# Both K ranges of the ups as seven products in a two-layer decoder trunk

## Chip, cores, metric

One core of one Trainium2 chip runs the whole program. The metric is the device time of one execution in microseconds. Engines: TensorE (PE) multiplies and writes PSUM, ScalarE (ACT), VectorE (DVE) and GpSimd (POOL) compute, SyncE (SP) issues most of the transfers. All arrays in memory are float32.

## What is computed

Two layers over 256 tokens of width 2048: a mixer and a SwiGLU feed-forward part with a residual each. The mixers aren't touched. The feed-forward part of each layer is

```
FFN_HIDDEN = 5632
def swiglu(h, w_gate, w_up, w_down):
    return (jax.nn.silu(h @ w_gate) * (h @ w_up)) @ w_down
h = rms_norm(x, ffn_norm[layer])
x = x + swiglu(h, w_gate[layer], w_up[layer], w_down[layer])
```

## The kernel before

**Numbers.** Every float32 operand is split in two halves that the fast matmul format holds: hi is the operand rounded, lo is the operand minus hi. A product of two operands is hi*hi + hi_w*lo_a + lo_w*hi_a, three matmuls in place of one.

**Slots.** The weights are read as blocks of 512 rows by 512 columns (1 MB), held as 128 x 2048. Each use of a block or of a sum of blocks is a *slot*. For slot t the SP queue loads the block into a place, ACT casts it to hi (`prepare`, line 807), DVE makes lo (line 1173), and PE multiplies. hi and lo have three places each, so the cast of slot t waits until PE has used slot t - 3, and on ACT and DVE `prepare(s + 3)` stands behind what belongs to step s. The blocks themselves lie in four places of `raw` and two of `work`; a load waits until the lo that frees its place is made.

**Units.** The hidden width is 11 units of 512 columns. The feed-forward part of each layer runs in five groups: FIRST (the first unit, steps g and h, and a pair of units), three times MIDDLE (a pair each), and LAST (a pair). What happens in a group is a list of steps, written out by hand at the top of the file; it sets the order on every engine. In it a0 to a5 and b0 to b5 with x0 and x1 are the gate projection of the pair, u, q and r the up projection, e, d and D the down projection (of the first unit, of the pair before, of the last pair), and T0, T1, t0, t1 are *turns*: PE transposes a finished unit, ACT rounds it to hi, DVE takes lo.

**Seven products.** For a pair of units, two halves of the tokens (128 each) and two K tiles of 512, the output is a 2 x 2 product of blocks, W11 to W22 of the weights. It is computed with seven products in place of eight: the products use W11, W22, W21 and sums of blocks, and the results are combined by small DVE operations of 128 x 512 (`gates`, `ups`) and kept in PSUM banks. The K range of 2048 is two such ranges: a is the first (K rows 0 to 1023) and b the second, x0 and x1 the seventh product of each. A product is one slot with 12 matmuls of 512 columns. A *wide* slot (g, h, e, d, D, q, r, v, w) uses one block for both token halves, with 24 matmuls.

The ups of FIRST and MIDDLE use seven products for the first K range only (u0 to u6); the second is done with four wide slots (q0, q1, r0, r1). The ups of LAST are eight wide slots (v, w).

**Sums of blocks.** DVE adds blocks in place right after the lo of slots 0, 1 and 3 of a range (line 1180). For a and b the sums with W12 are made by transfers from POOL's queue that add to the block in SBUF (`add_block`, line 759); for u W12 is loaded plainly and DVE adds it (`ADDED_BY_DMA`, `SOURCE`, `w12_loaded`). Per MIDDLE that is 33 slots, 8 sums on DVE, 25 loads from SP and 4 adding transfers from POOL.

**Waits that matter.** Small DVE operations of a group wait until PE has used their slot. T0 and T1 wait for the last of them that their unit needs. The down steps d00 and on wait until the turned unit is taken (`turn_taken`).

## Time and profile before

| | us |
|---|---|
| median of 3 runs | 1890.61 (1890.18 to 1891.11) |
| profiled execution | 1890.08 |
| its span | 1888.3 |
| PE busy | 1879.0 (100%) |
| PEld (weight loads) busy | 1583.5 (84%) |
| DVE busy | 1528.4 (81%) |
| ACT busy | 1000.2 (53%) |
| POOL busy | 80.0 (4%) |
| DMA | 414.49 MB, mean 220 GB/s |

Busy time is the time in which at least one instruction of the engine runs. A matmul's duration reaches over the start of the next one, so that the distance of two starts tells what one costs; on DVE too the next operation starts a little before the last has ended.

### The profile page before, as it was taken

The page shows a single profiled execution, that of the slowest core. Times are in us where ns is not written, and L with a number is a line of the kernel's source. Part 1 is how long each engine was busy: PE and PEld are TensorE (multiplying, and loading weights), DVE is VectorE, ACT ScalarE, POOL GpSimd, SP SyncE. Part 2 cuts the span into 40 slices and gives each one's busy share as a digit, 9 for nine tenths or more (in the row PEclk, how much of TensorE's full clock was granted, in tenths as well). Part 3 has the DMA queues.
Part 4 walks back from the last instruction along what each step waited for, and adds up shares of the span by engine and source line. Part 5 has one row for each costly group of instructions (what it writes and reads, how often), then busy time and mean ns, then how long its engine had stood idle before and what let it go on. Part 6 is the DMA issues. An engine that isn't in the chain of part 4 may idle for free.

```text
span 1888.3 us, 22147 instructions
## 1 busy us (share of the span) xinstructions
PE 1879.0 (100%) x9142; PEld 1583.5 (84%) x9142; DVE 1528.4 (81%) x1139; ACT 1000.2 (53%) x771; POOL 80.0 (4%) x125
## 2 busy tenths in 40 slices
PE   9999999999999999999999999999999999999998
PEld 8889999988888888888888888888888888888886
DVE  6656788966699899898897757889989899898855
ACT  6444344445555565555554536756565565555534
POOL 1000000000000000001000400010000000000000
PEclk9999999999999999999999999999999999999999
DMA  9555445355697868878878755497986868868762
GB/s 305 194 175 174 146 155 161 140 190 167 195 286 246 231 223 266 254 250 221 278 223 239 249 203 179 161 229 256 261 287 226 228 223 263 251 249 235 246 228 89
DMA packets 231772, 414.49 MB, mean 220 GB/s; under 512 B 6449, under 2 KB 55682, under 8 KB 231426
## 3 DMA queue, kind: packets, MB, share of 16 engines
q1 hardware_dynamic: 210336, 370.71, 56.3%
q0 software_dynamic: 21120, 41.95, 13.2%
q8 instruction: 67, 1.10, 0.2%
q10 hardware_dynamic: 226, 0.55, 0.1%
q14 instruction: 23, 0.19, 0.0%
HBM read 411.08 MB, written 2.10 MB: 219 GB/s over the span
## 4 chain that ended last, share of the span: by engine, by line
PE 97%; DVE 1%; DMA 1%; ACT 0%; issue 0%; SPq 0%; DVEq 0%; ACTq 0%
PE main L1844 28%; PE main L1850 14%; PE aux L1866 11%; PE main L1786 8%; PE main L1866 7%; PE aux L1870 6%; PE main L1788 4%; PE main L1870 3%; PE main L2083 3%; PE aux L2083 3%; PE main L2089 2%; PE aux L2089 1%; PE aux L1961 1%; PE aux L1793 1%; PE main L1894 1%; PE main L1893 1%
## 5 line engine op out<-in xcount | busy, mean ns | idle before, releaser
L807 ACT CAST hi<-raw 128x2048 fp32r<-128x2048 f32 (+1 forms) x328 | 624.5, 1907 | 503.1 <-PE main L1850 227.6
L1173 DVE TENSOR_TENSOR lo<-raw,hi 128x2048 fp32r<-128x2048 f32 x255 | 581.1, 2288 | 119.6 <-ACT hi L807 119.5
L1844 PE MATMUL main<-hi,mid 128*128 128x512 f32 x1632 | 387.8, 390 | 0.5 <-ACT hi L807 0.5
L1844 PEld LDWEIGHTS main<-hi,mid 128*128 128x128 f32 x1632 | 305.5, 188 | 63.9 <-issue 0.9
L807 ACT CAST hi<-work 128x2048 fp32r<-128x2048 f32 (+2 forms) x102 | 191.2, 1877 | 145.7 <-PE main L1850 26.6
L1173 DVE TENSOR_TENSOR lo<-work,hi 128x2048 fp32r<-128x2048 f32 x97 | 221.6, 2286 | 43.7 <-ACT hi L807 43.7
L1786 PE MATMUL main<-act,hi 128*128 128x512 f32 x640 | 226.6, 397 | 0.0
L1165 DVE TENSOR_TENSOR lo<-raw,hi 128x2048 fp32r<-128x2048 f32 x71 | 162.4, 2290 | 71.8 <-ACT hi L807 71.8
L1850 PE MATMUL main<-lo,mid 128*128 128x512 f32 x816 | 201.6, 389 | 0.0
L1850 PEld LDWEIGHTS main<-lo,mid 128*128 128x128 f32 x816 | 153.2, 188 | 31.8
L1788 PE MATMUL main<-act,lo 128*128 128x256 f32 x640 | 178.5, 279 | 0.0
L1844 PE MATMUL main<-hi,act 128*128 128x512 f32 x688 | 164.3, 391 | 0.0
L1844 PEld LDWEIGHTS main<-hi,act 128*128 128x128 f32 x688 | 128.4, 188 | 26.6 <-DVE act L1481 0.3
L1786 PEld LDWEIGHTS main<-act,hi 128*128 128x128 f32 x640 | 120.0, 188 | 26.5
L1866 PE MATMUL aux<-hi,act 128*128 128x512 f32 x544 | 136.1, 392 | 0.0
L1788 PEld LDWEIGHTS main<-act,lo 128*128 128x128 f32 x640 | 120.7, 189 | 0.3
L1866 PEld LDWEIGHTS aux<-hi,act 128*128 128x128 f32 x544 | 100.9, 188 | 20.2
L759 POOL DMA_DIRECT2D raw<-in_ffn_w_gate x31 | 40.0, 1290 | 1489.0 <-DVE lo L1173 1282.2
L1850 PE MATMUL main<-lo,act 128*128 128x512 f32 x344 | 85.0, 389 | 0.0
L1214 DVE TENSOR_TENSOR xn<-xn,main 128x1024 f32<-128x1024 f32 x55 | 66.8, 1215 | 20.6 <-PE main L1850 20.6
L1180 DVE TENSOR_TENSOR raw<-raw 128x2048 f32<-128x2048 f32 x32 | 73.0, 2285 | 6.8 <-DMA raw<-in_ffn_w_up 3.5
L1850 PEld LDWEIGHTS main<-lo,act 128*128 128x128 f32 x344 | 64.6, 188 | 13.4
(210 smaller groups left out, 2295.8 us busy)
## 6 DMA issues: line engine op xcount, KB each, us to landing
raw<-in_ffn_w_up SPq DMA_DIRECT2D x73, 1024.0 KB, 5.9
raw<-in_ffn_w_gate SPq DMA_DIRECT2D x63, 1024.0 KB, 7.0
raw<-in_ffn_w_down SPq DMA_DIRECT2D x58, 1024.0 KB, 6.6
raw<-in_ab_w_in SPq DMA_DIRECT2D x55, 1024.0 KB, 5.1
raw<-in_ffn_w_gate POOLq DMA_DIRECT2D x31, 1024.0 KB, 9.1
work<-in_ffn_w_down SPq DMA_DIRECT2D x30, 1024.0 KB, 7.5
work<-in_ffn_w_gate SPq DMA_DIRECT2D x25, 1024.0 KB, 8.0
work<-in_ffn_w_up SPq DMA_DIRECT2D x23, 1024.0 KB, 7.5
```

What stands on the lines that cost most here:

```text
L807: return nc.scalar.copy(out_, in_)
L1165: V.tensor_tensor(lo[:, s.place, :], raw[:, s.place, :], hi[:, s.place, :].bitcast(F32), ALU.subtract).then_inc(lo_ready, 1)
L1173: V.tensor_tensor(lo[:, split_at(t), :], raw_of[p.at], hi[:, split_at(t), :].bitcast(F32), ALU.subtract).then_inc(lo_ready, 1)
L1180: V.tensor_tensor(raw_of[a.at], raw_of[a.at], raw_of[b.at], ALU.add).then_inc(sum_made, 1)
L1214: V.tensor_tensor(xs, xs, bank_, ALU.add).then_inc(job_emptied, 1)
L1786: mm(bank(job)[:, c, :], hi[:, s.place, at:at + P], rhs[:, k0 + n, :, :], start=(first and n == 0), stop=False)
L1788: ins = mm(bank(job)[:, c, TOKENS:], lo[:, s.place, at:at + P], rhs[:, k0 + n, 0, :], start=False, stop=(last and n == depth - 1))
L1844: mm(o2[:, h, :], lhs[:, k0 + n, c, h * P:(h + 1) * P], w_hi, start=(first and c == 0 and n == 0), stop=False)
L1850: ins = mm(o2[:, h, :], lhs[:, k0 + n, 0, h * P:(h + 1) * P], w_lo, start=False, stop=(last and n == 3))
L1866: mm(o, a[c][:, n, :], hi[:, at, n * WIDE:(n + 1) * WIDE], start=(first and c == 0 and n == 0), stop=False)
L1870: ins = mm(o, a[0][:, n, :], lo[:, at, n * WIDE:(n + 1) * WIDE], start=False, stop=(last and n == 3))
L2083: mm(banks[:, h, :], act[:, k0 + n, c, h * P:(h + 1) * P], w_hi, start=(start[h] and c == 0 and n == 0), stop=False)
```

## The change

- The ups of all groups run as seven products over both K ranges: u0 to u5 over the first, y0 to y5 over the second, z0 and z1 the seventh products. q, r, u6, v and w are gone. Their products go to the same six banks as those of the gates, and `full_ups` combines them with 11 small operations (12 before in FIRST and MIDDLE, 4 in LAST).
- W12 of a is now loaded plainly and added by DVE (four sums on DVE); b, u and y are added by DMA (two sums on DVE each).
- W21 stays in its place unchanged: the sum for slot 5 is made in the place of W11, and x0, x1, z0 and z1 use the block that is loaded for slot 5 of the same range, without a load of their own.
- T1 (and t1) write to other banks than T0 (t0), and a3 and a4 wait for T1 to be taken, the first d waits for T0 only.
- The three lists of steps are new. Per MIDDLE there are 36 slots, 10 sums on DVE, 21 loads from SP and 6 adding transfers from POOL.

In the whole program the 512-column matmuls go from 7152 to 7008, the 128 x 2048 operations on DVE from 479 to 543, such casts on ACT from 409 to 445, and POOL's transfers from 40 to 60.

```diff
-FIRST = ("g0 g1 g2 g3 h0 h1 h2 h3 a0 T0 a2 b0 e0 a1 b2 e1 b1 a3 a4 e2 b3 a5 b5 x0 x1 b4 e3 u2 r0 u0 q0 "
-         "u1 u6 u3 q1 u4 u5 r1").split()
-MIDDLE = ("T0 a0 a2 T1 b0 b2 d00 d01 a1 x0 d10 b1 d11 a4 d20 a3 a5 x1 b3 d21 b5 b4 d30 d31 u0 u2 q0 u1 "
-          "q1 u6 u3 r0 u5 u4 r1").split()
-LAST = ("T0 a0 a2 T1 b0 b2 d00 a1 d01 a3 a5 d10 d11 b1 x0 d20 a4 d21 x1 b3 b4 b5 d30 v0 d31 v1 w0 v2 "
-        "v3 w1 t0 w2 w3 D00 t1 D10 D01 D11 D20 D21 D30 D31").split()
+FIRST = ("g0 g1 g2 g3 a0 h0 a2 a1 b0 a3 h1 a5 a4 b2 h2 b1 x0 h3 x1 T0 b3 u0 b5 b4 e0 y0 u1 z0 u2 u3 e1 "
+         "y1 u5 y2 y3 z1 u4 e2 y5 e3 y4").split()
+MIDDLE = ("a0 T0 a2 b2 d00 T1 a1 b0 a4 x0 a3 d01 a5 b1 d10 x1 b3 d11 u0 b4 b5 y0 d20 u1 u2 u3 z0 u5 d21 "
+          "y1 y2 y3 z1 d30 y5 u4 d31 y4").split()
+LAST = ("a0 T0 b0 T1 a1 d00 a2 a3 x0 a5 b1 b2 x1 b3 d01 b5 u0 a4 y0 b4 d10 d11 u1 u2 u3 z0 u5 y1 d20 "
+        "y2 y3 z1 y5 u4 d21 y4 d30 t0 d31 D00 t1 D10 D01 D11 D20 D21 D30 D31").split()
...
-ADDED_BY_DMA = ("a", "b")
-SOURCE = {k: "002025" if k in ADDED_BY_DMA else "0020W5" for k in "abu"}
+ADDED_BY_DMA = ("b", "u", "y")
+W21_STAYS = True
+SOURCE = {k: "002" + ("02" if k in ADDED_BY_DMA else "0W") + ("0" if W21_STAYS else "5") for k in "abuy"}
+RAW_W21 = {"x0": "a5", "x1": "b5", "z0": "u5", "z1": "y5", "u6": "u5"}
+W21_IN = {"a": ("x0",), "b": ("x1",), "u": ("z0", "u6"), "y": ("z1",)}
...
+def loaded_at(step):
+    return RAW_W21.get(step, step) if W21_STAYS else step
...
                 if step[1] == "3":
                     loaded(w21)
                     ve.wait_ge(sum_made, SUMS[g.pair, k, 3])
-                    add(w21, w11)
+                    if W21_STAYS:
+                        add(w11, w21)
+                    else:
+                        add(w21, w11)
...
+                def full_ups(g, s):
+                    due, r = g.up_due, g.up0
...
+                    if s == due[4]:
+                        used(g, "y4")
+                        ve.wait_ge(up_ready, r + 4)
+                        minus(kept_b, bank_p7, kept_b).then_inc(up_ready, 1)
+                        ve.wait_ge(up_ready, r + 5)
+                        minus(bank_q5, bank_q5, kept_b).then_inc(up_ready, 1)
+                    if s == due[6]:
+                        used(g, "y5")
+                        ve.wait_ge(up_ready, r + 6)
+                        plus(kept_b, kept_b, bank_q4).then_inc(up_ready, 1)
+                        ve.wait_ge(up_ready, r + 7)
+                        ve.wait_ge(gate_sig, g.sig("g01"))
+                        scaled(g01, kept_b, norm, 1, g01).then_inc(up_ready, 1)
...
-                            pe.wait_ge(turn_taken, T_HIDDEN[layer] + g.a)
+                            pe.wait_ge(turn_taken, T_HIDDEN[layer] + g.a - 1)
...
-                        pe.wait_ge(up_ready, t.before.up0 + (8 if i == 0 else 12))
-                        turn_hidden(layer, t.a - 2 + i, i, bank_b)
+                        pe.wait_ge(job_emptied, t.before.j + 4)
+                        pe.wait_ge(up_ready, t.before.up0 + (8 if i == 0 else UP_OPS[t.before.ups]))
+                        turn_hidden(layer, t.a - 2 + i, i, bank_a if i else bank_b, i)
...
+                    elif kind == "y":
+                        product(s, banks_full[i], operand(1, i), False, True)
+                    elif kind == "z":
+                        if i == 0:
+                            pe.wait_ge(up_kept, g.nth("u0") + 1)
+                        product(s, bank_x, a_tiles(2 * i + 1, 0), i == 0, i == 1)
```

The order on DVE at the end of a MIDDLE in layer 0 and the start of the next. L1173 (L1202 in the changed kernel) makes lo, L1180 (L1209) a sum of blocks, L1214 (L1246) a residual, L1449 (L1481) takes a turned unit, the 128x512 rows combine products. Before:

```order
L1620 TENSOR_TENSOR work<-main,work 128x512
L1620 TENSOR_TENSOR aux<-aux,work 128x512
L1623 TENSOR_TENSOR work<-work,main 128x512
L1512 SCALAR_TENSOR_TENSOR work<-work,small 128x512
L1173 TENSOR_TENSOR lo<-raw,hi 128x2048
L1623 TENSOR_TENSOR work<-work,aux 128x512
L1512 SCALAR_TENSOR_TENSOR work<-work,small 128x512
L1623 TENSOR_TENSOR work<-work,aux 128x512
L1512 SCALAR_TENSOR_TENSOR work<-work,small 128x512
L1449 TENSOR_TENSOR mid<-main,mid 128x4x256
L1173 TENSOR_TENSOR lo<-work,hi 128x2048
```

and after, from the sum behind the lo of a0:

```order
L1209 TENSOR_TENSOR work<-work,raw 128x2048
L1246 TENSOR_TENSOR xn<-xn,main 128x2x512
L1202 TENSOR_TENSOR lo<-raw,hi 128x2048
L1652 TENSOR_TENSOR work<-main,work 128x512
L1652 TENSOR_TENSOR aux<-aux,work 128x512
L1655 TENSOR_TENSOR work<-work,aux 128x512
L1544 SCALAR_TENSOR_TENSOR work<-work,small 128x512
L1655 TENSOR_TENSOR work<-work,aux 128x512
L1544 SCALAR_TENSOR_TENSOR work<-work,small 128x512
L1544 SCALAR_TENSOR_TENSOR work<-aux,small,work 128x512
L1202 TENSOR_TENSOR lo<-work,hi 128x2048
L1481 TENSOR_TENSOR mid<-main,mid 128x4x256
```

The four operations that T0 waits for had a slot of their own and were followed by a lo; now all seven stand together behind the last slot y4, with a sum and a residual ahead of them.

The order on DVE at the start of LAST in layer 0, behind the small operations. Before:

```order
L1449 TENSOR_TENSOR mid<-main,mid 128x4x256
L1173 TENSOR_TENSOR lo<-raw,hi 128x2048 x2
L1449 TENSOR_TENSOR mid<-main,mid 128x4x256
L1173 TENSOR_TENSOR lo<-work,hi 128x2048
L1173 TENSOR_TENSOR lo<-raw,hi 128x2048
L1180 TENSOR_TENSOR raw<-raw 128x2048
```

and after:

```order
L1202 TENSOR_TENSOR lo<-work,hi 128x2048
L1209 TENSOR_TENSOR work<-work,raw 128x2048 x2
L1481 TENSOR_TENSOR mid<-main,mid 128x4x256
L1202 TENSOR_TENSOR lo<-raw,hi 128x2048
L1481 TENSOR_TENSOR mid<-main,mid 128x4x256
L1202 TENSOR_TENSOR lo<-raw,hi 128x2048
```

The take of T0 moved behind the lo of a1 and two sums.

The order on DVE in the first steps of FIRST in layer 0. L1489 (L1521) makes the four sums of the activations, L1505 (L1537) their lo. Before:

```order
L1173 TENSOR_TENSOR lo<-raw,hi 128x2048
L1489 TENSOR_TENSOR work<-work 128x4x128 x4
L1173 TENSOR_TENSOR lo<-raw,hi 128x2048
L1505 TENSOR_TENSOR lo<-work,hi 128x1024 x2
L1173 TENSOR_TENSOR lo<-raw,hi 128x2048 x4
```

and after:

```order
L1202 TENSOR_TENSOR lo<-raw,hi 128x2048
L1209 TENSOR_TENSOR raw<-raw 128x2048
L1521 TENSOR_TENSOR work<-work 128x4x128 x4
L1202 TENSOR_TENSOR lo<-raw,hi 128x2048
L1537 TENSOR_TENSOR lo<-work,hi 128x1024 x2
L1202 TENSOR_TENSOR lo<-raw,hi 128x2048 x2
L1209 TENSOR_TENSOR raw<-raw 128x2048 x2
L1202 TENSOR_TENSOR lo<-raw,hi 128x2048 x2
```

Three sums came in between (one for a0, two for a1), and the slots they belong to are products.

## Rows read from the trace of the kernel before

**Rows 1.** Busy time, then slices of the span with the granted clock.

```profile
PE 1879.0 (100%) x9142; PEld 1583.5 (84%) x9142; DVE 1528.4 (81%) x1139; ACT 1000.2 (53%) x771; POOL 80.0 (4%) x125
...
PEclk9999999999999999999999999999999999999999
```

**Rows 2.** The chain that ended last, share of the span by engine.

```profile
PE 97%; DVE 1%; DMA 1%; ACT 0%; issue 0%; SPq 0%; DVEq 0%; ACTq 0%
```

**Rows 3.** Two MIDDLEs: length, busy PE, PEld, DVE, ACT, POOL, clock, DMA share, GB/s.

```profile
610.30:734.50 124.20, 124.20 (x559) 103.02 (x557) 111.04 (x67) 68.81 (x42) 5.13 (x4) 1.00 0.81 247
...
858.70:982.90 124.20, 124.20 (x558) 103.02 (x557) 110.93 (x67) 68.83 (x42) 5.16 (x4) 1.00 0.79 246
```

**Rows 4.** PE's timeline: a product, a wide slot, a turn (start, duration, instruction).

```profile
486.18 3.79 PE L1844 MATMUL main<-hi,act 128*128 128x512 f32 x16
...
884.22 1.98 PE L1866 MATMUL aux<-hi,act 128*128 128x512 f32 x8
886.04 1.07 PE L1870 MATMUL aux<-lo,act 128*128 128x512 f32 x4
886.94 3.79 PE L1844 MATMUL main<-hi,mid 128*128 128x512 f32 x16
890.57 1.98 PE L1850 MATMUL main<-lo,mid 128*128 128x512 f32 x8
892.38 1.07 PE L1866 MATMUL aux<-hi 128*128 128x512 f32 x4
...
900.54 1.98 PE L1866 MATMUL main<-hi,mid 128*128 128x512 f32 x8
...
982.15 1.04 PE L1793 MATMUL main<-ident,work 128*128 128x128 f32 x8
982.94 2.09 PE L1866 MATMUL aux<-hi,act 128*128 128x512 f32 x8
```

**Rows 5.** DVE's timeline: lo, sum, residual, and small operations.

```profile
927.69 1.22 DVE L1214 TENSOR_TENSOR xn<-xn,main 128x1024 f32<-128x1024 f32 x1
928.82 2.28 DVE L1173 TENSOR_TENSOR lo<-work,hi 128x2048 fp32r<-128x2048 f32 x1
...
935.74 2.28 DVE L1173 TENSOR_TENSOR lo<-raw,hi 128x2048 fp32r<-128x2048 f32 x1
937.94 2.28 DVE L1180 TENSOR_TENSOR raw<-raw,work 128x2048 f32<-128x2048 f32 x1
940.14 2.28 DVE L1173 TENSOR_TENSOR lo<-raw,hi 128x2048 fp32r<-128x2048 f32 x1
...
978.39 0.68 DVE L1620 TENSOR_TENSOR work<-main,work 128x512 f32<-128x512 f32 x1
...
981.31 2.28 DVE L1173 TENSOR_TENSOR lo<-raw,hi 128x2048 fp32r<-128x2048 f32 x1
```

**Rows 6.** ACT's timeline: a cast behind PE, with its idle time and what ended it.

```profile
900.80 1.91 ACT L807 CAST hi<-raw 128x2048 fp32r<-128x2048 f32 x1 [3.53 <-PE main L1850]
```

**Rows 7.** POOL's adding transfers: issue in ns, then landing.

```profile
L759 POOL DMA_DIRECT2D raw<-in_ffn_w_gate x31: 1282/1282/1438, 501.9 to 1752.2; - x31
...
DMA to landing us min/median/max: 8.5/9.0/11.0
```

**Rows 8.** SP's loads between 859 and 983.

```profile
DMA to landing us min/median/max: 5.2/7.6/9.3
```

**Rows 9.** DVE's timeline at the start of layer 0's FIRST.

```profile
482.03 2.86 DVE L1489 TENSOR_TENSOR work<-work 128x512 f32<-128x512 f32 x4
484.81 2.28 DVE L1173 TENSOR_TENSOR lo<-raw,hi 128x2048 fp32r<-128x2048 f32 x1
487.01 2.35 DVE L1505 TENSOR_TENSOR lo<-work,hi 128x1024 fp32r<-128x1024 f32 x2
```

**Rows 10.** ACT's timeline there.

```profile
486.95 1.28 ACT L1035 ACT_TABLE_LOAD   x1
488.25 1.27 ACT L1035 ACTIVATE work<-main,small 128x512 f32<-128x512 f32 x2
```

More of the change, by code:

```diff
@@ L122, in pair, with earlier, nth @@
         return PAIRS_OF_UNITS * self.layer + self.n
[L124 to L125 removed]
     @property
     def ups(self):
[L129 removed]
+        return "full" if "y0" in self.at else "half" if "u0" in self.at else "plain"
+    @property
+    def earlier(self):
+        return [g for groups in LAYERS for g in groups if g.pair < self.pair]
+    def nth(self, step):
+        return sum(step in g.at for g in self.earlier)
     @property
     def up0(self):
[L133 removed]
+        return sum(UP_OPS[g.ups] for g in self.earlier)
     @property
@@ L262, in places @@
                 continue
-            take(s, last_use(g, step, s), layer)
+            loads = loaded_at(step)
+            if g.at[loads] not in out:
+                take(g.at[loads], last_use(g, loads, s), layer)
             if w12_loaded(step):
```

156 lines of the change are left out of this document (101 added, 55 removed).

## The prediction

> **What bounds the kernel now.** I read the busy shares first: TensorE is busy for 1879.0 of 1888.3 us at full granted clock [rows 1]. The chain that ended last is 97% PE [rows 2]. Then the stretches of one middle group of the feed-forward part: 124.20 us long, PE busy in all of it, DVE for 110.9 us, ACT for 68.8 us [rows 3]. So the end is set by the number of matmuls, and DVE is second with 13.3 us of idle time in 124.2. There are six such groups (three in each layer), and a first and a last one in each layer. The PE rows give the unit of account: a product (12 matmuls) takes 886.94 - 884.22 = 2.72 us, its first eight 1.82; a wide slot (24 matmuls) takes 892.38 - 886.94 = 5.44 us, its first sixteen 3.63; a turn (8 transposes) 0.79 [rows 4]. One matmul of 512 columns is 5.44 / 24 = 0.2267 us. On DVE a lo or a sum of two 128x2048 blocks costs 2.20 us from start to start (935.74, 937.94, 940.14), a residual add 1.13, and the four small operations before the last turn 981.31 - 978.39 = 2.92 [rows 5]. ACT starts the cast of a slot about 0.26 us after PE has gone on (900.80 against PE's 900.54) and takes 1.91 [rows 4, 6].
>
> **What the change takes off PE.** In first and middle groups the ups were 7 products and 4 wide slots, 7 x 12 + 4 x 24 = 180 matmuls; now they are 14 products, 168. In the last group they were 8 wide slots, 192; now 168. Per layer 4 x 12 + 24 = 72 matmuls go, 144 in all. At 0.2267 us that is 32.6 us, if PE never waits. That alone would give 1858.0 us.
>
> **What it puts on the other engines.** The 14 products need 14 slots where there were 11 (in the last group 8), and every slot needs a cast on ACT and a lo on DVE. A middle group goes from 33 slots to 36. The sums of blocks on DVE go from 8 to 10 (four for the first gate block, whose W12 is now loaded plainly, two each for b, u and y). That is five more 128x2048 operations, 5 x 2.20 = 11.0 us, less one small add (0.7). DVE's busy time becomes 110.9 + 11.0 - 0.7 = 121.2 us [rows 3, 5]. PE's becomes 124.2 - 2.7 = 121.5. **The two engines are level**: the 13.3 us of slack on DVE shrink to 0.3, and lo can only run three slots ahead, so DVE also has to idle wherever it has caught up. ACT gets 3 casts, 68.8 + 5.7 = 74.5 of 121.5 us, and is no bound. Over a whole layer DVE still has room in the first and the last group (wide slots give PE 5.44 us for one lo), but only on average.
>
> Transfers become fewer: a middle group loads 21 blocks and adds 6 by DMA, 27 against 25 + 4 = 29. The W21 blocks of x0, x1, z0, z1 aren't loaded twice. SP's queue is therefore shorter. Its tightest load is that of W21 for x1: it may start when the lo of d01 is made and has to be cast three slots later. The loads landed in 5.2 to 9.3 us, median 7.6 [rows 8]; in the walk below DVE has about 9.5 us of other work there, of which the cast takes 1.9, so the median just fits. POOL's adds landed in 8.5 to 11.0 us after an issue of 1.28 [rows 7]; between the lo of b0 and that of b1 DVE has 14 us of other work, and 1.3 + 9.0 + 1.9 = 12.2 fits too. I take both at nothing and keep +1.5 us a group for the range. The longer life of the W21 buffers shows only in when loads may start, and is in this. The other banks for the second turn cost nothing by themselves.
>
> **Where PE waits now.** I walked the new orders by hand with the durations above, always taking the later of DVE's own queue and what it waits for. Four places come out.
>
> (1) *T0 of every group behind a full one* (eight times). y4 is the last step, and all seven small operations of the ups hang on it. In front of them DVE has from the end of u4: signal and cast 0.26 + 1.94, lo of a0 2.20, its sum 2.20, the residual of d31 1.13, lo of a2 2.20, then four small ones 2.92, and about 0.15 until PE reacts: 13.0 us. PE in the same time has d31, y4 and a0: 5.44 + 2.72 + 2.72 = 10.9. So T0 waits **2.1 us**; before, the operations for the first turn were done one slot earlier, and the turn stands at 982.15 with no idle in front [rows 4]. 8 x 2.1 = 16.8. Behind the first group DVE arrives 0.7 later still, twice: 1.4.
>
> (2) *d00 of the last group* (twice). T0's lo half now stands on DVE behind the lo of a1 and two sums. After y4: small ones until 6.8, lo 9.0, two sums 13.4, take 14.5. PE has a0, T0, b0, T1, a1 and would be at 11.9: **2.7 us** each, 5.4 in all. In the middle groups two slots lie in between and nothing waits.
>
> (3) *b0 of the first group.* a0, a1 now come between the wide slots, so three sums fall on DVE just as it makes the sums of the activations. Layer 0: those and their halves end at 491.5 (487.01 + 2.3 before [rows 9], plus one sum of 2.2); the cast of a2 ends at 493.6, behind the cast of those sums, ACT's table load and two activations, 1.28 + 1.27 [rows 10]; then lo a2, lo a1, two sums, lo b0, 5 x 2.20, give 504.6. PE, which leaves g3 at 486.18 [rows 4] and then has a0, h0, a2 and a1 (13.6), has done a1 at 499.8 and its hi part at 501.6: **3.1 us**. In layer 1 the same chain starts later and costs 1.1 (a0, for the activation sums) and 2.9.
>
> (4) *z1 of the first group*: from b4 to z1 DVE has four sums, five small operations and two residuals beside its lo, against 3.2 us of slack in each of only two wide slots, and is about 0.3 us late: 0.6.
>
> Sum of waits: 16.8 + 1.4 + 5.4 + (3.1 + 1.1 + 2.9) + 0.6 = 31.3; with half a microsecond for resumed matmuls, 31.8. Gain 32.6. **Net -0.8 us.** The profiled execution took 1890.08 us (span 1888.3 and 1.8 around it), 0.5 below the median of the runs, so the forecast is 1890.6 - 0.8 = **1889.8 us**.
>
> **A page against the rows.** The start-to-start time of 2.20 us [rows 5] is what the sum goes by. The Trainium skill ("VectorE: DVE Perf Modes", The TRN2 errata, and The DRAIN you can't avoid) gives (N+151)/0.96 ns for an fp32 tensor_tensor, 2291 ns at N=2048, and says that the next operation doesn't start until the pipeline is empty. This trace shows that duration (2.28) but operations that start 0.08 earlier. As an estimate from the page, 46 operations would cost 4.0 us more a group, DVE would need 125 us and the middle groups would be slower than before; by the rows they need 121.2. That result is part of the second rival.
>
> **The rivals.** *PE keeps most of the gain* (faster). For it: none of the waits is on record anywhere, and each is a difference of two sums near 12 us; if DVE gets through (1) and (3) half as late, (16.8 + 7.1) / 2 = 12 us come back: 1878. Full success would be 1858, which needs DVE to idle less than 0.3 us in 121; I give that almost nothing. Against it: (1) is a chain of five operations in one queue, each with its row. It decides where DVE's lag at y4 is under 1.9 us less than in my walk.
>
> *DVE is the bound all through the middle groups* (slower). Mechanism: each time DVE waits for a cast whose block hasn't landed (x1 after a load of 9.3 instead of 7.6 us: 1.7; d01: 1.3) the loss isn't made up, since in the walk only some 1.8 us of idle stand at y5, d31 and y4 in a period of 123.6. Above 1.8 us of such idle, or with DVE operations 1.5% dearer, every microsecond is paid: 3.0 - 1.8 = 1.2, six times, 7.2 and about 3 in first and last groups: 1900. For it: DVE at 98%. Against: fewer transfers than before, and the DMA share of 0.79 to 0.81 in these stretches [rows 3] falls with them.
>
> *POOL is starved.* Six DMAs a group come from POOL instead of four while DVE is nearly full. The rows show POOL's issue at 1282 ns in the median, 1438 at most, with DVE at 89% [rows 3, 7]. Were each held for one DVE operation (2.2 us), b1 and u1 would come about 2 us late in each group: 8 groups, 1.5 us each, 1902. The Trainium skill ("SBUF — State Buffer", SBUF: two separate sides) states such a lock for DVE operations in a two-port mode; the flat 1282 ns speaks against it for these.
>
> *The waits nearly cancel the gain* is the forecast itself.
>
> **How the numbers follow.** Forecast (1886.8 to 1894.4) 0.40; PE keeps a good part (1870 to 1886.8) 0.29; DVE the bound (1894.4 to 1910) 0.27; POOL starved 0.04. About 0.2% (3.8 us) is what a measurement of this kernel can tell from no change. Between 1886.8 and 1894.4 I put 0.40, below 0.29, above 0.31. The range for 8 in 10: 1878 (half of (1) and (3) gone) to 1902 (the two slow rivals).
>
> **What would show it.** 144 matmuls fewer. Middle groups of 123.6 us from T0 to T0 (121.5 if PE never waits, 126 and more if DVE is the bound), DVE busy about 121 in each. Idle on PE in front of the transposes that follow a group's a0 (2 us, ended by a small DVE operation), in front of the last group's first wide slot (2.7 us), in the first group's b0 (3 us, ended by a lo). ACT's casts waiting on DMA in front of x1 would show the second rival, POOL issues above 1.3 us the third. The prediction is wrong if DVE idles 5 us or more in a middle group, or if PE waits in places not named here.

## The result and the profile after

The changed kernel took 1902.08 us (median of 3 runs, 1899.76 to 1905.29) against 1890.61 before: ratio 1.0063, 95% interval 1.0049 to 1.0076. The 1902.08 us are 12.3 above the forecast and just above the upper end of its range. In the whole case three single executions were far longer (2653.82 and 2938.25 us, and 6190.1 of the kernel before); the ratios leave them out, and they move no median by more than 0.12 us. The profiled execution took 1899.76 us, 9.7 more than that of before. Its page, with the lines that answer to [rows 1, 2] (busy times, granted clock in slices, and the chain that ended last):

```profile
PE 1858.8 (98%) x8998; PEld 1558.9 (82%) x8998; DVE 1668.1 (88%) x1209; ACT 1066.1 (56%) x801; POOL 103.3 (5%) x145
...
PEclk9999999999999999999999999999999999999999
...
PE 75%; DVE 16%; DMA 4%; ACT 3%; issue 2%; DVEq 0%; SPq 0%; ACTq 0%
```

PE has 144 matmuls fewer (by form the two profiles hold 7348 and 7204 matmuls of 512 columns, 495 and 559 operations of 128 x 2048 on DVE and 423 and 459 such casts: more than stated with the change, with the same differences). But its busy time fell by 20.2 us and not by 32.6, and its idle time (span less busy) rose from 9.3 to 39.4 us. The three middle groups of layer 0 from T0 to T0 (columns as in [rows 3]: length, busy PE, PEld, DVE, ACT, POOL, clock, DMA share, GB/s), where the length before was 124.20:

```profile
618.69:742.79 124.10, 122.00 (x544) 100.53 (x545) 120.66 (x70) 74.17 (x44) 7.70 (x6) 1.00 0.80 229
742.79:867.10 124.31, 122.00 (x545) 100.56 (x545) 120.48 (x70) 74.03 (x44) 7.72 (x6) 1.00 0.80 228
867.10:992.39 125.29, 123.29 (x544) 101.93 (x545) 120.81 (x70) 74.10 (x44) 8.97 (x7) 0.99 0.80 227
```

The groups are as long as before with a product less in them, and DVE is busy for 120.5 to 120.8 us, 9.7 more. From the start of layer 0's FIRST to the T0 behind it, it took 146.0 us and now 155.1; from LAST's T0 to the same transpose in layer 1's mixer it took 218.5 and now 213.0. An a0 (2.72 us) that stood behind the T0 now stands ahead of it, so 2.7 us of both differences are only that shift; LAST lost 24 matmuls (5.4 us) besides.

PE's timeline shows the waits, in brackets behind the row: b0 of FIRST in layer 0, two of the T0, and d00 of LAST in both layers.

```profile
504.73 1.20 PE L1945 MATMUL aux<-lo,act 128*128 128x512 f32 x4 [2.96 <-DVE lo L1202]
...
739.71 1.07 PE L1945 MATMUL aux<-lo,act 128*128 128x512 f32 x4
742.79 1.06 PE L1868 MATMUL main<-ident,work 128*128 128x128 f32 x8 [2.01 <-issue]
...
867.10 1.30 PE L1868 MATMUL main<-ident,work 128*128 128x128 f32 x8 [2.00 <-issue]
868.05 3.55 PE L1941 MATMUL aux<-hi,mid 128*128 128x512 f32 x8
...
1002.32 3.93 PE L1919 MATMUL main<-hi,mid 128*128 128x512 f32 x16 [2.50 <-DVE mid L1481]
...
1733.34 3.94 PE L1919 MATMUL main<-hi,mid 128*128 128x512 f32 x16 [0.88 <-DVE mid L1481]
```

The last row is the same d00 in layer 1, which waits 0.88 us and not 2.50; the reason comes below. At T0 the profile names no releaser ("issue"); the fourth small operation on DVE ends at 742.69 (741.94 + 0.75, in the rows of DVE below), 0.1 us before T0 starts.

The row at 868.05 is the one to learn from. Eight matmuls that take 1.98 us elsewhere took 3.55. The window around it, and that behind b0, with the clock in the last column but two:

```profile
865.00:872.00 7.00, 5.00 (x20) 4.13 (x20) 6.72 (x8) 2.81 (x2) 0.00 (x0) 0.76 0.00 0
...
503.00:510.00 7.00, 5.27 (x16) 4.18 (x17) 7.00 (x4) 2.49 (x3) 1.44 (x1) 0.76 0.55 159
```

A mean of 0.76 in 7.00 us is 3.4 us at half the clock (1.2 in place of 2.4 GHz). There are four such stretches, behind b0 of FIRST (layer 0) and three of the eight T0. Work that is done in one takes 1.7 us longer. The slices of the page round to 9 and hide them. The last stretch lies behind the T0 at 1723.40, just ahead of layer 1's d00: PE came there 1.7 us late while DVE's chain went on, and d00's wait was shorter by that much (0.88 for 2.50). So a stretch costs nothing where the next wait takes it up.

DVE's queue ahead of the T0 at 742.79:

```profile
731.94 2.29 DVE L1202 TENSOR_TENSOR lo<-raw,hi 128x2048 fp32r<-128x2048 f32 x1 [0.43 <-ACT hi L836]
734.15 2.29 DVE L1209 TENSOR_TENSOR raw<-raw 128x2048 f32<-128x2048 f32 x1
736.35 1.22 DVE L1246 TENSOR_TENSOR xn<-xn,main 128x1024 f32<-128x1024 f32 x1
737.48 2.29 DVE L1202 TENSOR_TENSOR lo<-raw,hi 128x2048 fp32r<-128x2048 f32 x1
739.68 0.69 DVE L1652 TENSOR_TENSOR work<-main,work 128x512 f32<-128x512 f32 x1
...
741.94 0.75 DVE L1544 SCALAR_TENSOR_TENSOR work<-work,small 128x512 f32<-128x512 f32 x1
```

This is the chain of the prediction, operation for operation: lo, sum, residual, lo, four small ones without a gap.

### The profile page after: what moved, and what is told of

Its sections match the earlier page's. It is cut to its first block, busy times and chain, and to the rows that moved or that the text cites. A ratio compares the mean times of both kernels' runs of the same rounds, so it can differ in the third digit from the quotient of the medians.

```text
span 1898.2 us, 22037 instructions
## 1 busy us (share of the span) xinstructions
PE 1858.8 (98%) x8998; PEld 1558.9 (82%) x8998; DVE 1668.1 (88%) x1209; ACT 1066.1 (56%) x801; POOL 103.3 (5%) x145
## 4 chain that ended last, share of the span: by engine, by line
PE 75%; DVE 16%; DMA 4%; ACT 3%; issue 2%; DVEq 0%; SPq 0%; ACTq 0%
PE main L1919 19%; PE aux L1941 13%; PE main L1925 10%; DVE lo L1202 8%; PE main L1861 8%; PE aux L1945 7%; PE main L1941 5%; PE main L1863 4%; PE main L1945 3%; DVE raw L1209 3%; ACT hi L836 2%; DMA raw<-in_ffn_w_gate 1%; DVE work L1209 1%; PE aux L2036 1%; PE aux L1868 1%
## 5 line engine op out<-in xcount | busy, mean ns | idle before, releaser
L836 ACT CAST hi<-raw 128x2048 fp32r<-128x2048 f32 (+1 forms) x349 | 665.1, 1909 | 459.8 <-PE main L1925 221.0
L1202 DVE TENSOR_TENSOR lo<-raw,hi 128x2048 fp32r<-128x2048 f32 x276 | 627.6, 2290 | 57.4 <-ACT hi L836 56.8
L1919 PE MATMUL main<-hi,mid 128*128 128x512 f32 x1632 | 388.9, 390 | 5.0 <-DVE mid L1481 3.4
L1202 DVE TENSOR_TENSOR lo<-work,hi 128x2048 fp32r<-128x2048 f32 x112 | 255.8, 2287 | 11.0 <-ACT hi L836 11.0
L1941 PE MATMUL aux<-hi,act 128*128 128x512 f32 x960 | 238.8, 391 | 0.0
L1194 DVE TENSOR_TENSOR lo<-raw,hi 128x2048 fp32r<-128x2048 f32 x71 | 162.4, 2290 | 71.6 <-ACT hi L836 71.6
L1941 PEld LDWEIGHTS aux<-hi,act 128*128 128x128 f32 x960 | 180.9, 189 | 37.7
L1925 PEld LDWEIGHTS main<-lo,mid 128*128 128x128 f32 x816 | 153.2, 188 | 31.8
L1945 PE MATMUL aux<-lo,act 128*128 128x512 f32 x480 | 129.5, 391 | 7.3 <-DVE lo L1202 7.2
L1863 PEld LDWEIGHTS main<-act,lo 128*128 128x128 f32 x640 | 120.7, 189 | 0.3
L1945 PEld LDWEIGHTS aux<-lo,act 128*128 128x128 f32 x480 | 89.9, 188 | 28.5 <-DVE lo L1202 10.1
L1209 DVE TENSOR_TENSOR raw<-raw 128x2048 f32<-128x2048 f32 x48 | 109.3, 2288 | 0.0
L1919 PE MATMUL main<-hi,act 128*128 128x512 f32 x432 | 103.5, 392 | 1.7 <-DVE act L1513 1.7
L1919 PEld LDWEIGHTS main<-hi,act 128*128 128x128 f32 x432 | 80.5, 188 | 18.6 <-DVE act L1513 2.1
L1941 PE MATMUL aux<-hi,mid 128*128 128x512 f32 x320 | 83.0, 403 | 0.0
L1941 PE MATMUL main<-hi,mid 128*128 128x512 f32 x320 | 80.5, 395 | 0.0
```

Of the source, the lines that this page charges most:

```text
L836: return nc.scalar.copy(out_, in_)
L1194: V.tensor_tensor(lo[:, s.place, :], raw[:, s.place, :], hi[:, s.place, :].bitcast(F32), ALU.subtract).then_inc(lo_ready, 1)
L1202: V.tensor_tensor(lo[:, split_at(t), :], raw_of[p.at], hi[:, split_at(t), :].bitcast(F32), ALU.subtract).then_inc(lo_ready, 1)
L1209: V.tensor_tensor(raw_of[a.at], raw_of[a.at], raw_of[b.at], ALU.add).then_inc(sum_made, 1)
L1863: ins = mm(bank(job)[:, c, TOKENS:], lo[:, s.place, at:at + P], rhs[:, k0 + n, 0, :], start=False, stop=(last and n == depth - 1))
L1919: mm(o2[:, h, :], lhs[:, k0 + n, c, h * P:(h + 1) * P], w_hi, start=(first and c == 0 and n == 0), stop=False)
```

## Experiments

Times are medians on the device; each batch was compared with the kernel before on the same chip (1890.2 to 1890.6).

**The change again**, five rounds.

> The changed kernel as it is, on the same chip as the next three. Theory A (waits on DVE plus clock drops): 1899 to 1905 us, some 30 us of idle on TensorE at the same places (2.0 us in front of the transposes behind a group's a0, 3.0 and 2.6 in the first groups' b0, up to 2.5 at the last groups' first wide slot), and a number of half-clock stretches of 3.4 us that differs from run to run, so a spread of several us where the kernel before has under 1. Theory B (DVE is the bound all the time, the clock is of no account): the same idle, but the time of every run within 1 us of the others.

1902.86 us (1901.24 to 1904.97), ratio 1.0066 [1.0053, 1.0079]. Most waits are the same to a few hundredths; small ones at z0 and d10 differ by 0.3 to 0.6 us, and d00 of layer 1, which had no slow stretch ahead of it this time, waited 2.49. Stretches at half clock again, partly at other places: behind b0 (twice as long), one T0 in each layer, and d00 of layer 1. So the long waits are nearly fixed, and which of them costs clock is not. Theory A.

**Filler products in T0's wait.**

```diff
                         pe.wait_ge(job_emptied, t.before.j + 4)
+                        if i == 0:
+                            for n in range(30):
+                                mm(bank_b[:, 0, 0:P], ones_r[:], ones_r[:], start=True, stop=True)
                         pe.wait_ge(up_ready, ...)
```

> Adds 30 matmuls of 128 columns (ones by ones, into the bank that the turn overwrites) in front of each T0 of the middle and last groups, where TensorE waits 2.0 to 2.2 us; nothing is left out. They take some 1.8 us, so they fit into the wait. Theory A: TensorE isn't idle there, so the clock is not lowered behind a T0 (3 of the 4 drops of the first profile lay there); each drop avoided gives back about 1.5 us: 2 to 6 us below the changed kernel, 1896 to 1899, and a smaller spread. Theory B, or clock drops that have nothing to do with idle time: the same time as the changed kernel within 1 us, or slower by a few tenths for each T0, and drops at the same places.

1902.99 us, ratio 1.0063 [1.0050, 1.0076], no difference to the change. PE's timeline:

```profile
865.96 1.07 PE L1945 MATMUL aux<-lo,act 128*128 128x512 f32 x4
866.86 3.46 PE L2280 MATMUL main<-ones_r 128*128 128x128 f32 x30
870.16 1.06 PE L1868 MATMUL main<-ident,work 128*128 128x128 f32 x8
870.98 2.09 PE L1941 MATMUL aux<-hi,mid 128*128 128x512 f32 x8
```

The fillers take 3.30 us in place of a gap of 2.17 (742.79 - 740.62), so they cost 1.1 us at eight places, 9 us; no stretch at half clock is left behind a T0. PE's wait at d00 fell from 2.5 to 1.4 us, since PE came later. A cost and a gain of one size cancelled, so this run alone proved nothing (theory A had expected 1896 to 1899). Hence a shorter filler (16 in place of 30):

> As the run with 30 filler products ahead of the first turn (T0) of every full group, but with 16 (16 x 110 ns = 1.8 us), so that they take the place of most of the 2.0 us wait and of no more. The products fill a bank that is free then; nothing reads them. Theory A (waits of 2 us and more also bring half-clock stretches of 3.4 us behind them, at some 1.6 us each; T0 has up to three such stretches in a run of the changed kernel): the T0 waits shrink to about 0.2 us, no stretch at half clock stands behind a T0, and the time is 5 to 7 us below that of 30 fillers, which cost 1.1 us each over the wait that they covered: 1896 to 1898. Theory B (the period of a group is set by DVE's total, so what PE does in its wait is free, and the stretches at half clock are hidden in DVE's time): time as before the fillers, 1902 to 1903, in both sizes.

The five executions are the best evidence for the clock's price so far. Mean granted clock and time: 0.999 and 1896.15, 0.998 and 1899.20, 0.996 and 1901.37, 0.995 and 1903.12, 0.995 and 1903.60. The median, 1901.37, missed theory A's number, its lowest run hit it. The waits at b0 (2.94 and 2.57) and d00 (2.51 in both layers) had no filler; in the fastest execution, the profiled one, none of these four was followed by a stretch at half clock. With 22 fillers at b0 and 20 at d00 as well:

```diff
+                if filler:
+                    fill(filler)
                 pe.wait_ge(lo_ready, s + 1)
...
                         if i == 0 and m == 0:
+                            if g.final:
+                                fill(20)
                             pe.wait_ge(turn_taken, T_HIDDEN[layer] + g.a - 1)
```

> As the run with 16 filler products ahead of the first turn, and 22 more inside b0 of FIRST (in front of its lo part, 2.4 of its 2.9 or 2.6 us wait) and 20 ahead of d00 of LAST (2.2 of 2.5 us). They go to a bank that holds nothing then. So PE never waits longer than some 1.7 us in the feed-forward part, at the same places and the same lengths as in the changed kernel. Theory A (the half-clock stretches hang on waits of 2 us and more, and they make both the extra time and the spread of the changed kernel): no stretch at half clock in the feed-forward part, all executions within 2 us of each other, at 1895 to 1897, which is before (1890.3) + waits not paid by the fewer products. Theory B (the stretches come with the load, wherever PE stands): executions still spread by 5 us and more, median 1900 and up, stretches at other places.

1897.16 us (1896.14 to 1900.15), ratio 1.0036 [1.0022, 1.0050], clock 0.999 in all five. Around b0, and T0:

```profile
503.00:510.00 7.00, 6.47 (x39) 5.60 (x38) 7.00 (x5) 2.53 (x3) 1.44 (x1) 1.00 0.57 177
...
742.71 1.09 PE L1868 MATMUL main<-ident,work 128*128 128x128 f32 x8 [0.22 <-DVE work L1544]
```

The waits are still paid, as filler; only the clock is kept. So **5.7 us of the change's 12.6 (1902.86 - 1890.24) are clock**, and theory B falls; each of the two medians stands against its base within 2.6 us, so 5.7 is a size and not a fine figure. The spread of 4 us is larger than theory A said. In the slowest execution, the profiled one, the wide slot d10 waits 0.75 to 1.0 us for a residual in four groups; in the fastest run with 16 fillers such waits were 0.27, 0.86 and 0.52, and in the change 0.30 in one group. The chain that ends there, in the trace of the change (start, length, what):

```profile
759.56 13.27 DMA raw<-in_ffn_w_gate
...
772.86 1.92 ACT hi L836
...
774.80 2.29 DVE lo L1202
777.10 2.20 DVE raw L1209
779.30 1.14 DVE xn L1246
...
780.48 3.92 PE main L1919 x16
```

This is POOL's adding transfer for b1: b1's cast stood 1.70 us for it, and DVE idled 1.19. From the start of its issue it landed after 13.27 us here (wait of 0.30), 13.24, 13.81 and 13.46 us in the run with 16 fillers, and 13.72 to 13.95 us in the four groups of this run, and the wait follows it. What makes it land later is open.

**Other orders in FIRST and LAST.**

```diff
-FIRST = ("g0 g1 g2 g3 a0 h0 a2 a1 b0 a3 h1 a5 a4
+FIRST = ("g0 g1 g2 g3 h0 a0 h1 a2 a1 b0 a3 a5 a4
-LAST = ("a0 T0 b0 T1 a1 d00 a2 a3
+LAST = ("a0 T0 a2 b0 d00 T1 a1 a3
```

> New order of the first steps of the first group (g0 g1 g2 g3 h0 a0 h1 a2 a1 b0 a3 a5 a4) and of the last (a0 T0 a2 b0 d00 T1 a1 a3), everything else as in the changed kernel. Theory A: the waits there are local queues on DVE (sums behind the lo of a0 and a1 in front of the lo of b0; the take of T0 behind the lo of a1 and two sums). In the first group wide slots stand between, in the last the take comes before those sums, so 3.0 + 1.7 + 2.6 at the first groups and 2.5 + 0.9 at the last ones go, 10 us less or nearly, and one or two clock drops with them: 1888 to 1893. Theory B (DVE is short of time over the whole group, so that a wait taken away comes back at the next slots): under 3 us are gained.

1906.69 us, ratio 1.0086 [1.0073, 1.0099]. b0's wait went, and layer 0's first T0 came earlier, at 616.19 (620.57 in the change run again, with 6.8 us at half clock behind b0, and 618.69 in its first profile, with 3.4). d00's wait went too, but a3 came to wait for the taking of T1:

```profile
512.02 2.08 PE L1941 MATMUL aux<-hi,act 128*128 128x512 f32 x8 [1.10 <-ACT hi L836]
...
1009.52 2.55 PE L1941 MATMUL main<-hi,mid 128*128 128x512 f32 x8 [2.66 <-DVE mid L1481]
```

In layer 1 the same two waits are 2.50 (for a cast, at 1245.69) and 4.28 us (at 1745.66). PE's idle time is no longer than in the change run again (40.4 against 41.9 us), but its busy time is (1864.7 against 1860.5), at a mean clock of 0.991 to 0.993 against 0.993 to 0.995. So the waits moved and the clock paid for it; theory A, 1888 to 1893, missed.

**W12 of b by DVE too**, two operations more in each group.

```diff
-ADDED_BY_DMA = ("b", "u", "y")
+ADDED_BY_DMA = ("u", "y")
```

> W12 of b too is loaded plainly and added by DVE: two more 128x2048 operations (4.4 us) on DVE in each group, 20 in all, two fewer transfers from POOL, one more load. DVE would need 120.6 + 4.4 = 125.0 us in a middle group that lasts 124.1. Theory that DVE's total bounds the middle groups: they grow to 127 to 129 us each, the kernel to 1925 to 1940. Theory that only the queue in front of T0 counts: b's sums lie in the middle of the group, the T0 chain is the same, and the groups stay at 124 to 125: 1902 to 1908.

1950.87 us, ratio 1.0321 [1.0303, 1.0339], above the ranges of both theories. DVE has 44 us more work in the program (20 sums) and the program is 48 us longer, of which 30 us are more idle time on PE and 17 more busy time, at a mean clock of 0.989 to 0.990. The first middle group, with DVE busy in 125.1 of 129.3 us:

```profile
623.05:752.30 129.25, 122.88 (x544) 100.32 (x545) 125.14 (x72) 73.97 (x44) 5.13 (x4) 1.00 0.70 212
```

**All W12 by DMA**, two DVE operations fewer in each group; then the same with a4 three places later; then with the orders of FIRST and LAST above.

```diff
-ADDED_BY_DMA = ("b", "u", "y")
+ADDED_BY_DMA = ("a", "b", "u", "y")
```

```diff
-MIDDLE = ("a0 T0 a2 b2 d00 T1 a1 b0 a4 x0 a3 d01 a5
+MIDDLE = ("a0 T0 a2 b2 d00 T1 a1 b0 a3 x0 d01 a4 a5
```

> The second turn of the up's step: W12 of the group's first gate block too is added by DMA, so that DVE has two operations of 2.2 us (4.4 us) fewer in every group and POOL issues eight adds per group and not six. Theory A (DVE's queue is late at single places because it has no slack; each saved operation gives back its wait): the T0 waits of 2.0 us and b0's of 3.0 go; but the row order of a middle group leaves a4's second half only two products behind a1, and its second added half lands some 4 to 5 us late, so a new wait of that size stands there, six groups of it: 1890 to 1905. Theory B (the 32 us of waits come from something other than DVE's two more operations): the T0 waits stay. Theory C (POOL is starved of its port by DVE): the adds issue slower than 1.28 us each, and waits stand before a4 and b-products of over 5 us.

> All W12 parts added by DMA, and the row order of the middle groups with a4 three products later (a0 T0 a2 b2 d00 T1 a1 b0 a3 x0 d01 a4 a5). DVE's own time of a middle group is 120.6 - 4.4 = 116.2 us against PE's 121.3. Theory A: T0's waits and that of b0 in FIRST go and nothing takes their place but small waits at the adds, so 24 to 30 us of idle PE and all half-clock stretches behind T0 go: 1865 to 1880, under both kernels. Theory B (the added halves come late, landing 9 us behind issue and eight in a row on POOL's queue): waits of 2 to 4 us at a3 or a4 in each group: 1885 to 1895.

> As the run with all W12 parts added by DMA and a4 later in the middle groups, and FIRST and LAST in the orders of the run that changed them alone (there they gained 4.4 us in FIRST and lost it in LAST, where the product behind T1 waited 2.7 to 4.3 us for DVE's take of the turned block). Theory A: with DVE's sums gone ahead of T1's take that wait shrinks to under 1 us, and this is 1 to 4 us below the run with the old FIRST and LAST. Theory B (T1's take is late by its own chain, not by the queue): the wait stays, and this is 0 to 4 us above it.

The first took 1927.75 us, ratio 1.0206 [1.0190, 1.0221]: a4 stood for its second added half, and for 4.2 to 5.1 us as foreseen. The total missed my range because theory A also had T0's waits go, which they didn't (1.90 each), and had no clock in it (0.988 to 0.991).

```profile
767.21 3.75 PE L1941 MATMUL main<-hi,mid 128*128 128x512 f32 x8 [5.00 <-ACT hi L836]
```

The second took 1887.84 us (1885.52 to 1889.61), ratio 0.9985 [0.9976, 0.9994], 15 us under the change. That is above theory A's range and inside theory B's, but without B's waits at a3 or a4, and the surprise is where the rest stays: **b0's wait is gone, but every T0 still waits 1.90 us**. A middle group, and DVE ahead of T0:

```profile
737.80:861.41 123.61, 121.71 (x545) 100.67 (x545) 116.76 (x68) 74.06 (x44) 10.26 (x8) 1.00 0.87 238
...
730.50 1.22 DVE L1246 TENSOR_TENSOR xn<-xn,main 128x1024 f32<-128x1024 f32 x1 [1.15 <-PE main L1925]
732.49 2.29 DVE L1202 TENSOR_TENSOR lo<-raw,hi 128x2048 fp32r<-128x2048 f32 x1 [0.78 <-ACT hi L836]
734.70 0.68 DVE L1652 TENSOR_TENSOR work<-main,work 128x512 f32<-128x512 f32 x1
```

DVE now idles for 1.15 and 0.78 us in the chain that was full: the lo ahead of the small operations (a2's) waits for its cast, which waits for PE to end d31, at 730.30. From there it is 0.25 and 1.94 for the cast, 2.20 for the lo and the same 3.1 us of small operations, 7.5 us, while PE has y4 and a0, 5.44. In the change that cast ended at 737.35 and DVE reached the lo at 737.48: this second chain had been hidden 0.1 us behind the first.

The third took 1898.05 us, ratio 1.0043 [1.0029, 1.0057], 10 us above the second where theory B had 0 to 4; in LAST the product behind T1 waited longer still ([4.13 <-DVE mid] at 1010.43), so that T1's taking, not DVE's load, is late there. That is theory B's mechanism; the mean clock is lower too (0.993 to 0.994 against 0.996 to 0.997).

**T0 one product later**, on the change, and on the all-DMA kernel with d00 later too.

```diff
-MIDDLE = ("a0 T0 a2 b2 d00 T1 a1
+MIDDLE = ("a0 a2 T0 b2 d00 T1 a1
```

```diff
-MIDDLE = ("a0 T0 a2 b2 d00 T1 a1 b0 a3 x0 d01 a4 a5
+MIDDLE = ("a0 a2 T0 b2 a1 d00 T1 b0 a3 x0 d01 a4 a5
-LAST = ("a0 T0 b0 T1 a1 d00 a2 a3
+LAST = ("a0 a2 T0 b0 T1 a1 d00 a3
```

> The changed kernel with T0 one product later in the middle groups (a0 a2 T0 b2 d00 instead of a0 T0 a2 b2 d00); nothing else moves. Theory A (the T0 wait is a matter of the row order: the operations that T0 needs come behind y4, only one product ahead of it, and everything behind depends on PE's own progress): the 2.0 us wait vanishes at the six T0 concerned, and d00, which now has one product less behind the turn, waits for the turned unit, 1 to 3.4 us. Net 1893 to 1904. Theory B (DVE's total, 120.6 us a group, bounds the group): T0 to T0 stays at 124.1 us whatever stands where.

> The run with all W12 parts added by DMA, which kept 1.9 us of wait at every T0 although DVE had two sums fewer: there DVE stands idle for 0.8 and 1.2 us ahead of the lo that precedes T0's operations, since that lo hangs on a cast that hangs on PE. So not DVE's load but the row order holds T0. Here T0 comes one product later (a0 a2 T0 b2 a1 d00 T1 b0 a3 x0 d01 a4 a5), d00 keeps its two products behind it, and LAST is a0 a2 T0 b0 T1 a1 d00. Theory A: no wait at T0, under 0.5 us at d00: 8 x 1.9 = 15 us and the half-clock stretches behind go: 1866 to 1874, 14 to 24 us under both kernels. Theory B (DVE's load holds PE somewhere whatever the order): the waits reappear at a1, d00 or T1 and the time stays above 1882.

1912.05 us (1.0108 [1.0092, 1.0124]) and 1899.84 us (1.0056 [1.0042, 1.0070]), both worse than their base and above theory A's ranges. The wait didn't go to d00 but came earlier and grew: a2 needs the bank that the ninth small operation frees.

```profile
746.21 0.96 PE L1941 MATMUL aux<-hi,mid 128*128 128x512 f32 x3 [2.75 <-DVE work L1655]
```

So T0 and a2, which were tried behind a0, both hang on y4's operations, and the steps ahead of a0 had to change.

**y4 ahead of the last wide slot**, on the change and on the all-DMA kernel (with a4 later).

```diff
-          "y1 y2 y3 z1 d30 y5 u4 d31 y4").split()
+          "y1 y2 y3 z1 d30 y5 u4 y4 d31").split()
```

(FIRST ends in y4 e3 likewise.)

> The changed kernel with its last two steps exchanged: y4 d31 in the middle groups and y4 e3 in FIRST, not d31 y4 and e3 y4. So a wide slot (5.44 us on PE) and a0 (2.72) lie between the product y4, on which seven small DVE operations hang, and T0 or a2. Theory A (row order: y4 last leaves only a0 between): T0 no longer waits, neither does a2 or the down step, six to eight times 2.0 us go with the half-clock stretches behind them: 1880 to 1888. Theory B (DVE's total of 120.6 us a group is the bound, and T0 is only where PE pays it): the same microseconds come back at another place of the group (a1, a4, b0), T0 to T0 stays at 124 us and the time at 1899 to 1903. The hand count puts DVE 1.5 us behind PE in the first ten steps of a group, so A is the likelier but with waits of about 1 us at a2 or b0.

> All W12 parts added by DMA, a4 three products later, and the last two steps exchanged as in the run before. Against the run with a4 later alone (1887.8, T0 waits of 1.9 us eight times = 15.3 us of idle PE, three half-clock stretches) theory A (row order) expects the T0 waits and the stretches behind them to go: 1887.8 - 15.3 - 3 x 1.6 = 1868, range 1864 to 1874, faster than the kernel before by over 1%. Theory B (DVE bound) is excluded in advance only in part, DVE's 116 us a group being 5 under PE's 121.3: by it the time stays above 1880.

1925.37 us (1.0183 [1.0169, 1.0197]) and 1889.71 us (0.9996 [0.9987, 1.0005]). The first is above the ranges of both its theories, the second above theory A's. T0 no longer waits for a small operation, but for the residual of d31, whose bank it takes, and that stands behind them. In the first PE is idle for 10 us more than in the change run again and busy for 10 more, at a mean clock of 0.986. T0 on the change, then by all DMA:

```profile
748.55 1.97 PE L1868 MATMUL main<-ident,work 128*128 128x128 f32 x8 [4.19 <-DVE xn L1246]
```

```profile
739.58 1.09 PE L1868 MATMUL main<-ident,work 128*128 128x128 f32 x8 [1.99 <-DVE xn L1246]
```

**Both orders together**: y4 ahead of d31 and T0 behind a2 (with a4 later in both), first with all W12 by DMA, then with DVE adding that of a as in the change.

> All W12 parts added by DMA, y4 ahead of the last wide slot, and T0 behind a2 in place of a0 (a0 a2 T0 b2 a1 d00 T1 b0 a3 x0 d01 a4 a5; LAST a0 a2 T0 b0 T1 a1 d00). In the run with y4 ahead of d31, T0 stood 2.0 us because it writes to the bank from which DVE first has to take d31's result, and that operation stands behind a lo; in the run with T0 behind a2 alone, a2 stood 2.65 us because the ninth small operation was not made. With both edits a2's operations are made by its start (735.4 against 736.1 in that trace) and T0's bank is empty by 739.5, while PE reaches T0 at about 740. Theory A (row order): no wait over 0.7 us at a0, a2, T0 or b2: 1889.7 - 8 x 2.0 - 4 stretches x 1.5 = 1868, range 1863 to 1876, over 1% under the kernel before. Theory B (something else makes a 2 us gap there in any order): a gap of 2 us at b2, a1, d00 or T1, and 1882 or more.

> The same two orders on the changed kernel, with W12 of a added by DVE as there (120.6 us of DVE a middle group, not 116.2). From the trace with y4 ahead of d31 alone DVE is in one unbroken queue from the sum of a0 on: small operations until 745.1, lo 747.3, residual 748.4, lo 750.6, while PE wants a2's lo part at 746.2 and T0 at 747.1. Theory A (load and order together): a2 waits 1.1, T0 1.3 and b2 or a1 up to 2 us, so 3 to 4 us a group stay: 1885 to 1905. Theory B (row order alone): it gains as much as the run beside it and comes to 1870 to 1880.

1882.24 us (1880.14 to 1883.77), ratio 0.9955 [0.9942, 0.9969]; and 1924.96, ratio 1.0182 [1.0164, 1.0201]. The two kernels differ in twenty DVE sums (44 us) and the adding transfers in their place, and by 42.7 us in time: 30 us of idle time on PE and 12 of busy time, with the mean clock at 0.992 to 0.994 against 0.998 to 0.999. The second missed both theories. In it d00 waits for the take of the turned unit in every group, which stands behind two sums:

```profile
757.83 3.94 PE L1919 MATMUL main<-hi,mid 128*128 128x512 f32 x16 [3.38 <-DVE mid L1481]
```

In the first, the longest waits are the same ones, at d00 (2.02 at 746.36, 2.13 at 1346.82), as its theory B had it, though DVE also idled 1.26 us there behind a cast that stood for its block; and no stretch at half clock is left in the feed-forward part. It gained 7.5 us on the run with y4 alone, a third of what I expected. With d00 behind T1 and b0, and d01 behind a5:

```diff
-MIDDLE = ("a0 a2 T0 b2 a1 d00 T1 b0 a3 x0 d01 a4 a5
+MIDDLE = ("a0 a2 T0 b2 a1 T1 b0 d00 a3 x0 a4 a5 d01
```

> The run with both orders and all W12 parts added by DMA, and in the middle groups d00 one product later, T1 two slots earlier and d01 behind a5: a0 a2 T0 b2 a1 T1 b0 d00 a3 x0 a4 a5 d01. There d00 waited 1.3 to 2.1 us and a3 0.56 us in each of six groups for DVE's take of the turned unit, and in one of the groups shown d01 waited 1.4 us for its block. Theory A (each wait left is one operation late by the row order): d00 and a3 no longer wait, 6 x (1.8 + 0.56) = 14 us go, and the time is 1882.2 - 14 = 1868, range 1865 to 1874. Theory B (the transfers: the later d01 and the longer life of the buffers make loads late, of which the cast of b2, which stood 4.2 us on ACT for its block, is a first sign): new waits on casts, 1876 to 1884. Theory C (it comes out slower again, over 1884), as T0 later did alone.

**1878.89 us (1878.12 to 1881.72), ratio 0.9942 [0.9928, 0.9955]**, the fastest kernel of the case, 11.6 us under the kernel before and 23 to 24 under the change. d00's wait in the middle groups is gone; b0 waits 0.39 to 1.64 us in its place, and d10 0.76 to 1.30 in three groups:

```profile
750.64 1.20 PE L1945 MATMUL aux<-lo,act 128*128 128x512 f32 x4 [1.64 <-DVE lo L1202]
```

Ahead of it in the same trace stands the cast of b2, late by its block, and DVE behind that cast:

```profile
740.82 1.91 ACT L836 CAST hi<-work 128x2048 fp32r<-128x2048 f32 x1 [4.42 <-DMA work<-in_ffn_w_gate]
...
742.76 2.29 DVE L1202 TENSOR_TENSOR lo<-work,hi 128x2048 fp32r<-128x2048 f32 x1 [1.52 <-ACT hi L836]
```

That speaks for theory B (transfers) as what is next; no run took it away, so this part is argued only.

## Why the prediction was wrong

**What held.** 144 matmuls fewer at 0.2267 us. DVE's 121.2 us a group (120.5 to 120.8). The places and most lengths of the waits, forecast and measured: T0 2.1 and 2.0 (1.9 behind FIRST); d00 of LAST 2.7 and 2.50, in layer 1 0.88 behind a slow stretch (2.49 without it); b0 of FIRST 3.1 and 2.96, in layer 1 2.9 and 2.57; the wait for the activations there 1.1 and 1.68; z1 0.3 and 0.56. Their sum was 31.3 us, and PE's idle time rose by 30.1. The 0.7 us more behind FIRST didn't come. Some 2.4 us of idle stand at places that the forecast didn't name: e3 (0.59 and 0.64), z0 of layer 1 (0.58), d10 (0.30) and a turn in LAST (0.30).

**The step that failed is what a wait costs.** The sum took PE "at full granted clock" throughout and "half a microsecond for resumed matmuls" in all. PE's busy time is 1858.8 us where 1879.0 - 32.6 = 1846.4 were due: 12.4 too many. Four stretches at half clock make 4 x 1.7 = 6.8. Busy time also grows at each stop, because the last matmul before it counts with its whole recorded duration and nothing overlaps its end: the gap at T0 is 742.79 - (739.71 + 0.907) = 2.17 us, of which the trace calls 2.01 idle. At some 20 stops that is 3 us. The forecast had half a microsecond for it. So -32.6 + 30.1 + 6.8 + 3 = +7.3 of the measured +9.7; about 2 us are not placed. The counts of stretches and stops are those of one execution. The forecast had -32.6 + 31.8. Without the low clock the change gives 1897.2 (the run with all waits filled), still above the forecast's own 1886.8 to 1894.4 but inside the range of 1878 to 1902. A second step failed on a smaller scale: POOL's adds were taken "at nothing", and the one for b1 held PE for 0.3 us in one group of the profiled execution and for up to 1.0 in other executions.

The Trainium skill ("TensorE: Matmul & The Clock Gate", HAM oscillation — how this bites in real kernels) describes the gate dropping to half rate in waits for DMA that recur between stretches of matmuls. These traces agree on the drop, here behind single waits of 1.8 to 5.1 us, most of them for DVE, but not one for one: of the eight T0 waits three were followed by it in one execution and two in the next. The prediction should have had it as a rival.

**The rivals.** *PE keeps most of the gain*: no, the long waits came out as walked. *DVE is the bound through the middle groups*, with 1900, is nearest. Its mechanism, casts late by transfers, is in the trace, but small: DVE idled 1.19 us behind b1's cast and PE 0.30. Its neighbour is larger: DVE's total is level with PE's, so that 44 us more on DVE cost 48 (W12 of b by DVE) and 44 us less, with fit orders, gave 42.7. That these figures are so alike is partly chance, since 17 us of the first and 12 of the second are busy time of PE, with the clock in it. *POOL starved*: no. The rows that answer to [rows 7], one group of its transfers and the landing of all sixty:

```profile
L788 POOL DMA_DIRECT2D raw<-in_ffn_w_gate x14: 1282/1282/1438, 505.0 to 1754.7; - x14
...
DMA to landing us min/median/max: 8.4/10.5/14.3
```

The issue takes 1282 ns as before; what grew is the landing, a median of 10.5 us where 9.0 stood. My 12.2 us for the chain to b1 (1.3, 9.0 and 1.9) was 15.2 in the group shown above (13.27 and 1.92), more than the slack of 14 us.

**The page on DVE's pipeline.** By the Trainium skill ("VectorE: DVE Perf Modes", The DRAIN you can't avoid) the prediction's estimate was 125 us of DVE in a middle group; the groups without a slow stretch took 124.1 to 124.3, with DVE busy 120.5 to 120.7, and starts stand 2.20 apart (731.94 + 2.21, 737.48 + 2.20). The same section says too that a next operation which isn't held starts earlier, and gives no figure there, so the rule as the prediction used it was only half of it. The rows decide for 2.20, and the time beyond 121.5 is in the waits that the timeline shows.

**How the two causes share the loss.** T0's wait looked like DVE's load, because that chain is the later of two 0.1 us apart, and the walk named only the one. Taking away two sums in each group left it (1.90 for 2.00), moving T0 alone made it worse, moving y4 alone turned it into another, and both moves paid only with the lower load. Against the change run again the lower load alone (with a4 placed to fit) gave 15.0 us, the orders alone lost 22, the two together gave 20.6 and, with d00 later, 24.0. No run moved a4 without taking the load away, so how much of the 15.0 is a4's place isn't shown; with the load away it was worth 40 us (1927.75 to 1887.84).

## What to carry over

Before you price the removal of one wait, work out the second latest chain at the same place, and what the engine then meets next. Price a wait of about 2 us on PE above its length: in this kernel 30 us of waits cost some 42, in good part through clock and stops, and a check is to fill the wait with idle matmuls of just its length. Where a change makes a second engine level with the first (121 of 121.5 us), don't count on orders until that engine has slack again: the four runs with new orders at full load were slower than the change, by 4 to 22 us. Here 4.4 us a group, moved to transfers, made the same orders go from 1925 to 1882 us.
